# PEER's v passes: TensorE's rows scaled in place by ScalarE and added with the identity, without diagonal matrices

## The reference

```python
def peer_ffn(x, w_q, sub_keys, u, v):
    ...
    expert_idx = jnp.take_along_axis(cand_i, top_pos, axis=-1)
    gates = jax.nn.softmax(top_s, axis=-1).astype(x.dtype)
    ...
    def expert_block(args):
        xb, eb, gb = args
        ub = jnp.take(u, eb, axis=0)
        act = jax.nn.gelu(jnp.einsum('thkd,td->thk', ub, xb), approximate=False)
        vb = jnp.take(v, eb, axis=0)
        return jnp.einsum('thk,thkd->td', gb * act, vb)
```

## Time and profile before

| | us |
|---|---|
| median of 3 runs | 2470.8 |
| lowest, highest | 2463.44, 2474.6 |
| the profiled execution, its own time | 2473.55 |
| its span (first to last instruction) | 2471.7 |
| mean granted TensorE clock, share of full speed | 0.802 |
| busy in the span: TensorE, VectorE, POOL, ScalarE | 1634.6, 1363.1, 993.7, 314.0 |

### The profile page before, as it was taken

The page is one execution under the profiler, slowest core; times in us unless marked ns, Lnnn a source line. Parts: engine busy times, 40 slices in busy tenths (PEclk is TensorE's granted clock), DMA queues, the critical chain, the costliest instruction groups (busy, mean ns, idle before and its releaser), DMA issues.

```text
span 2471.7 us, 16839 instructions
## 1 busy us (share of the span) xinstructions
PE 1634.6 (66%) x5324; PEld 983.4 (40%) x5324; DVE 1363.1 (55%) x2980; ACT 314.0 (13%) x756; POOL 993.7 (40%) x1049
## 2 busy tenths in 40 slices
PE   8989300086747448874655886301777998999997
PEld 6557300032215236322523632100222777778843
DVE  0132698857688864688785478897444154210002
ACT  1121000011112110111211011100111222110001
POOL 0000166666665545576555467676663100000000
PEclk9869755599967679987867998655999885699998
DMA  6304399989999999999999899999996761033421
GB/s 237 119 1 153 119 382 374 376 328 352 358 402 404 399 372 351 356 366 393 398 404 371 335 368 378 389 409 358 364 370 227 217 211 35 12 113 131 162 93 51
DMA packets 229369, 694.37 MB, mean 281 GB/s; under 512 B 21102, under 2 KB 35133, under 8 KB 228642
## 3 DMA queue, kind: packets, MB, share of 16 engines
q0 software_dynamic: 148576, 540.09, 57.2%
q1 hardware_dynamic: 80706, 153.22, 17.5%
HBM read 690.61 MB, written 2.62 MB: 280 GB/s over the span
## 4 chain that ended last, share of the span: by engine, by line
PE 44%; DVE 21%; issue 19%; POOL 7%; DMA 6%; another core or an unknown queue 2%; ACT 1%; DVEq 0%; SPq 0%; ACTq 0%; PEldq 0%; POOLq 0%
PE bank L271 41%; DVE ROWS L914 11%; POOL ROWS L869 6%; DMA ROWS<-in_peer_v,IDX 4%; DVE XP L918 3%; DMA ROWS<-in_peer_u,IDX 2%; PE bank L286 1%; DVE QP L1132 1%; DVE BI L1082 1%; PE bank L1188 0%; DVE X L426 0%; DVE TI L1082 0%; DVE EX L1138 0%; DVE BV L1079 0%
## 5 line engine op out<-in xcount | busy, mean ns | idle before, releaser
L271 PE MATMUL bank<-ROWS,DG 128*128 128x512 f32 (+1 forms) x1032 | 502.3, 625 | 292.5 <-issue 182.0
L869 POOL DMA_INDIRECT ROWS<-in_peer_u,IDX x512 | 485.0, 947 | 428.3 <-DVE ROWS L914 161.1
L869 POOL DMA_INDIRECT ROWS<-in_peer_v,IDX x512 | 492.1, 961 | 323.0 <-issue 141.1
L914 DVE SCALAR_TENSOR_TENSOR ROWS<-ROWS,XP 128x1024 f32<-128x1024 f32 x512 | 599.8, 1217 | 29.2 <-issue 23.7
L918 DVE SCALAR_TENSOR_TENSOR XP<-ROWS,GATE,XP 128x1024 f32<-128x1024 f32 x252 | 323.8, 1285 | 222.5 <-DMA ROWS<-in_peer_v,IDX 181.1
L271 PEld LDWEIGHTS bank<-ROWS,DG 128*128 128x128 f32 x1032 | 188.0, 196 | 599.6 <-issue 368.7
L271 PE MATMUL bank<-XT,ring 128*128 128x256 f32 (+2 forms) x1488 | 297.4, 360 | 24.7 <-issue 22.3
L271 PEld LDWEIGHTS bank<-XT,ring 128*128 128x128 f32 (+1 forms) x1488 | 259.9, 203 | 62.4 <-issue 34.3
L271 PE MATMUL bank<-ring,XT 128*128 128x512 f32 (+6 forms) x608 | 236.6, 550 | 26.4 <-issue 23.4
L354 POOL TENSOR_TENSOR stat<-stat,CN 128x2 f32<-128x2 f32 x5 | 3.5, 705 | 496.6 <-DVE stat L443 447.7
L271 PEld LDWEIGHTS bank<-ring,XT 128*128 128x128 f32 x608 | 117.4, 208 | 140.9 <-issue 131.4
(11 more groups left out here) (354 smaller groups left out, 1524.9 us busy)
## 6 DMA issues: line engine op xcount, KB each, us to landing
ring<-in_peer_w_q SPq DMA_DIRECT2D x12, 2048.0 KB
ring<-in_ple_w_gate SPq DMA_DIRECT2D x9, 2048.0 KB
ring<-in_a_w_in SPq DMA_DIRECT2D x6, 2048.0 KB
ROWS<-in_peer_u,IDX POOLq DMA_INDIRECT x512
ROWS<-in_peer_v,IDX POOLq DMA_INDIRECT x512
ring<-in_b_w_out SPq DMA_DIRECT2D x4, 2048.0 KB
ring<-in_ffn_w_gate SPq DMA_DIRECT2D x3, 2048.0 KB
ring<-in_ffn_w_up SPq DMA_DIRECT2D x3, 2048.0 KB
```

The source lines that it names most:

```text
L271: return mm(out_, lhsT, rhs, start=start, stop=stop, skip_group_check=True)
L869: G.indirect_dma_start(ROWBUF[slot(n, c)][:, :], None, tables[table], bass.IndirectOffsetOnAxis(IDX[:, tt, c:c + 1], axis=0)).then_inc(row ...
L914: V.scalar_tensor_tensor(row, row, 1.0, XP[:, :], ALU.mult, ALU.mult, accum_out=ACTV[:, tt, c:c + 1]).then_inc(row_used, 1)
```

## The change

ScalarE no longer makes diagonals. It waits until the row has landed, multiplies all its 1024 columns in place by the gate of each partition, and counts `row_scaled`. TensorE waits for that count alone and multiplies the identity by the scaled row, into the same banks. The four DG buffers and ScalarE's wait for `pe_used` are gone. POOL's waits, VectorE's rows and the order of the work on every engine stay. The diff:

```diff
--- before.py
+++ after.py
@@ -44,7 +44,6 @@
 NCAND = 4 * TOPK + (TOPK - 4) * 4
 SLOTS = 12
 VECTORS = 13
-DIAGS = 4
 
 NH, NKV, HD = 8, 2, 64
 CB, CS, NCMP, CHID = 32, 16, 15, 256
@@ -823,13 +822,12 @@
         IDX = sb("IDX", [P, TT, PICKS], I32, peer_mem)
         GATE = sb("GATE", [P, TT, PICKS], F32, peer_mem)
         ACTV = sb("ACTV", [P, TT, PICKS], F32, peer_mem)
-        DG = [sb(f"DG{i}", [P, P], F32, peer_mem) for i in range(DIAGS)]
         ROWBUF = [ROWS[:, s, :] for s in range(SLOTS)]
 
         passes = [(l, tt, table) for l in range(2) for tt in range(TT) for table in "uv"]
         row_in = [S(f"row_in{s}") for s in range(SLOTS)]
         row_used, picks_ready = S("row_used"), S("picks_ready")
-        pe_used, diag_ready = S("pe_used"), S("diag_ready")
+        pe_used, row_scaled = S("pe_used"), S("row_scaled")
         WAYS = 2
 
 
@@ -932,26 +930,25 @@
 
             accs = result("accA"), result("accB")
             for x, c in list(enumerate(pe_rows_of[n]))[x0:x1]:
-                PE.wait_ge(*arrived(n, c))
-                PE.wait_ge(diag_ready, tensor_used(n, x + 1))
+                PE.wait_ge(row_scaled, tensor_used(n, x + 1))
                 end = x == len(pe_rows_of[n]) - 1
-                d, row = DG[tensor_used(n, x) % DIAGS], ROWBUF[slot(n, c)]
-                last = mul(accs[0][:, :], d[:, :], row[:, 0:512], x == 0, end)
+                row = ROWBUF[slot(n, c)]
+                last = mul(accs[0][:, :], ident, row[:, 0:512], x == 0, end)
                 if end:
                     held.clear()
                     last.then_inc(bank_ready("accA"), 1)
-                    mul(accs[1][:, 0:256], d[:, :], row[:, 512:768], False, True).then_inc(bank_ready("accB"), 1)
-                    mul(accs[1][:, 256:512], d[:, :], row[:, 768:1024], False, True).then_inc(pe_used, 1)
+                    mul(accs[1][:, 0:256], ident, row[:, 512:768], False, True).then_inc(bank_ready("accB"), 1)
+                    mul(accs[1][:, 256:512], ident, row[:, 768:1024], False, True).then_inc(pe_used, 1)
                 else:
-                    mul(accs[1][:, :], d[:, :], row[:, 512:1024], x == 0, False).then_inc(pe_used, 1)
+                    mul(accs[1][:, :], ident, row[:, 512:1024], x == 0, False).then_inc(pe_used, 1)
 
         def act_share(n, x0=0, x1=PICKS):
 
             tt = passes[n][1]
             for x, c in list(enumerate(pe_rows_of[n]))[x0:x1]:
-                if tensor_used(n, x + 1) > DIAGS:
-                    A.wait_ge(pe_used, tensor_used(n, x + 1) - DIAGS)
-                A.activation(DG[tensor_used(n, x) % DIAGS][:, :], ident, ACT.Copy, scale=GATE[:, tt, c:c + 1]).then_inc(diag_ready, 1)
+                row = ROWBUF[slot(n, c)]
+                A.wait_ge(*arrived(n, c))
+                A.activation(row[:, :], row[:, :], ACT.Copy, scale=GATE[:, tt, c:c + 1]).then_inc(row_scaled, 1)
 
         def act_next_x(n):
 
```

## The result

Over 20 runs of each, the median is 2482.27 us after and 2473.86 before; the ratio is 1.0036, 95% interval 1.0022 to 1.0050. That is 8.9 us slower (5.4 to 12.4), in the direction and the range forecast, at a little over half of the 15.4 us that the sum gave. By the forecast's own boundary of 0.5% it is still "same", which had 0.40, and not "slower", which had 0.51. From pass 1's first matmul on a row to VectorE's last addition in pass 7 both traces take 1394.4 us (500.19 to 1894.61 before, 502.71 to 1897.08 after), and behind that addition, where no edit of this document reaches, the fourteen traces take anything from 566.0 to 577.7 us.

The account below looks back on a forecast made before the run. It took TensorE to bound the routing steps and gathers to set pass 7's pace. Terms 7.5 + 0.75 + 1.3 − 3.2 + 9.1 = +15.4 on the profiled 2473.55 gave 2489.0, at the runs' median 2486 us; range 2465 to 2510.

Parts of the forecast that it names:

- Routing steps: Passes 3 and 5: the first row of each of ten steps waits 0.75 us longer for ScalarE, +7.5 us.
- Starts and tails: Pass 7's first row +0.75 us and last row +1.3, both now behind ScalarE's scaling; ends of passes 3 and 5, 0.
- Tail of pass 1: Last rows no longer wait for a diagonal held by a late count; TensorE ends at 673.7 instead of 676.9, −3.2 us.
- The slot ring: Row slots are given back 1.3 us later, lengthening seven single POOL stalls in pass 7 by 1.3 each, +9.1 us.
- The ring is bound by latency: Rival, chance 0.22: half of the 43 turns over the row slots 1.3 us longer, +34, 2505 us; all, 2533.
- Freed starvation: Rival, chance 0.15: TensorE's stops behind late diagonals are on the path, so 13.4 us come back, about 2464 us.
- The ring has slack: Rival, chance 0.18: pass 7's stalls leave the DMA queue supplied; only steps, starts and tails remain, +6.4, 2477 us.
- Not what it says: Rival, chance 0.02: TensorE keeps the identity and skips weight loads, making its rows cheaper, about 2477 us.
- Traffic of ScalarE beside the gathers: ScalarE rewriting 512 KB a row beside DMA writes was claimed to cost 0.
- The ACTIVATE: ScalarE's scaling of one row was taken as 1.15 us, 0.75 more than making a diagonal.

Follow-up runs that it names:

- Others_scaled: Kernel before, with diagonals kept in the 60 step rows of passes 3 and 5 and the other 196 rows scaled in place: ratio 1.0008, +2.0 us.
- diag8: Kernel before with eight diagonal buffers in place of four, nothing scaled: ratio 0.9989, −2.7 us.
- double_scale: Changed kernel with each row outside the steps written twice by ScalarE, a plain copy then the scaling: ratio 1.0030 against the kernel before, +7.1 us.

## Why the prediction was right, point by point

- **The number.** The range held the time of the kernel before as well, so that 2482.3 fell into it proves little. That the sum came near is in part luck: two terms were wrong with opposite signs, +9.1 and −3.2, and the three others make 9.55, close to the 8.9.
- **Routing steps, +7.5.** Right in mechanism, and in size as far as it can be told: 0.65 to 0.80 more idle ahead of the first rows in the trace of pass 3, and +7.7 us (3.7 to 11.6) with the step rows alone scaled. Its own text had the condition too, that TensorE bounds the steps while the DMA has slack. Where the DMA is full the steps are 0.68 longer each and most of that is absorbed behind them; no cost shows in the time (0.9995), which the forecast had as its lower bound of 0.
- **Starts and tails.** The end of pass 7 is as reckoned: VectorE's wait grew by 1.17. Its start can't be read in the 2470 condition, where POOL's stall there is 7.14 before, 4.68 after and 6.3 to 7.3 in the six other traces; in the 2370 condition it is 0.82 longer than with a diagonal. In pass 3 the slack of 2.3, which the forecast counted on, was gone in this trace: VectorE waited 0.68 at L969. In pass 5 TensorE's last row still ended ahead of VectorE (1531.71 and 1533.35), but VectorE then stood 1.77 us for a late count. Others_scaled holds all of these together, +2.0 with a wide interval, so their sizes are confirmed by brackets alone.
- **Tail of pass 1, −3.2.** In the profile it came as forecast (TensorE's end 674.85, forecast 673.7; L969 at 674.89, 2.1 earlier). As a term it was wrong: what ended pass 1 late is a late count, and VectorE waits for one too. Taking ScalarE's wait away doesn't take that away; in the six other traces of the 2470 condition that cost 3.6 to 10.5 us.
- **The slot ring, +9.1: the step that failed.** It said that seven stalls of pass 7 would each be 1.3 longer. After the change pass 7 has, past its start, five POOL gaps over 1 us, 17.4 us together, where there were nine with 22.3, and its first matmul to L969 takes 172.2 us against 173.7. The other rows together cost 2.0 us. I had treated the lateness as a fixed time added to the matmul's end; the counts come late in bursts, and a matmul that ends 1.3 later mostly has its count arrive with the same burst. That the counts come in bursts the traces show, and that POOL's gathers at 1796.58 and 1832.94 follow one; that this is why nothing is lost is an argument. That the cost isn't there shows in pass 7's length too, from its first matmul on a row to its last: in the five traces with its rows scaled it is 171.7 to 175.5 us, mean 173.4, in the three with diagonals 172.9 to 173.6, mean 173.2. Without this term the sum is +6.4, and the measured 8.9 lies between.
- **Rivals.** "The ring is bound by latency" (2505) is out by others_scaled. "Freed starvation" (2464) is out by the measured time itself, and by diag8 as far as the full 13.4 go. "The ring has slack" (2477), given 0.18, was nearest to the truth in mechanism, and the measured 2482.3 lies between it and the forecast. "Not what it says" is out: the weights are loaded as often as before.
- **Traffic of ScalarE beside the gathers** at 0: holds. In the 2370 condition 256 rows written in place ran at ratio 0.9995.
- **The ACTIVATE, 1.15.** Right: 1.144. The two rows behind it were read too kindly: the prediction said that the trace agrees with the rule of the Trainium skill, page "ScalarE: Activation LUTs", section "What ACT_TABLE_LOAD costs", in slope and in its 0.13, but 1.06 and 0.27 give 0.88 ns a column against the page's 0.833, and 0.13 stands against its 0.093. In double_scale 1.056 without and 1.146 with the vector scale put it at 0.09.

## What to carry to other kernels

When a cheap operation is replaced by a costlier one on an idle engine, count the places where that engine stands between two pieces of work of the engine that sets the pace: here, by the best values, the 60 rows of the steps carried four fifths of the price, and of these probably the ten first rows nearly all. Then look whether that engine could have done it earlier in its own order: with three rows made ahead of a copy no cost was left. A wait in the trace behind a count that came late isn't a stable term of a sum: look at several traces before you give it a number.

## What the runs showed of the hardware that was not expected

The same kernel on the same chip took 2370.7 and 2464.4 us in two batches, 4% apart. In the slower condition the projections' matmuls have gaps of up to 1.1 us between them with nothing that they are seen to wait for, and counts of TensorE reach VectorE, ScalarE and POOL up to 10 us late, in bursts; in the quicker one neither occurs. The mean granted clock hardly tells the two apart (0.79 to 0.81 in the runs of the one, 0.80 to 0.81 in those of the other), though in the step windows it is 0.93 after the change in the one and 1.00 in the other. What brings it about was not tried. A change measured in only one of the two conditions can come out as +0.36% or as nothing.
